# Differential attention on one Trainium2 core: another order of the same work on four engines, and 12 of 40 copies per head moved from ScalarE to VectorE

## The reference

```python
def diff_attention(q, k, v, lam, subln_g, lambda_init):
    ...
    def block(args):                       # 128 queries at a time
        qi, idx = args
        q_chunk = (idx * Q_BLOCK + jnp.arange(Q_BLOCK)) // CHUNK
        sc = jnp.einsum('bhqd,bhkd->bhqk', qi, kt).astype(jnp.float32) * (HEAD_DIM ** -0.5)
        mask = key_chunk[None, :] <= q_chunk[:, None]
        sc = jnp.where(mask[None, None], sc, NEG)
        p = jax.nn.softmax(sc, axis=-1).reshape(b, h, 2, Q_BLOCK, s)
        a = p[:, :, 0] - lam * p[:, :, 1]
        return jnp.einsum('bhqk,bhkv->bhqv', a.astype(vt.dtype), vt)
    ...
    o = rms_norm(o, subln_g) * (1.0 - lambda_init)
```

## Time and profile before

| | us |
|---|---|
| median of 3 runs | 2486.18 (2485.43 to 2487.39) |
| the profiled execution | 2485.43, of which the span of the trace is 2483.6 |
| `diff_attn` in it, first scores to last norm | 598.5 to 983.9: 385.4 |
| head 1, from its first scores to those of head 2 | 690.1 to 783.8: 93.7 |

### The profile page before, as it was taken

How to read it: one execution, slowest core, us unless ns; L and a number is a source line. 1 busy time by engine, 2 the same in 40 slices (tenths; PEclk the granted TensorE clock), 3 DMA queues, 4 the chain that set the end, 5 groups by cost and what they waited for, 6 DMA issues and landing times.

```text
span 2483.6 us, 34874 instructions
## 1 busy us (share of the span) xinstructions
PE 2358.0 (95%) x11796; PEld 1962.1 (79%) x11796; DVE 1589.1 (64%) x3041; ACT 1216.3 (49%) x2779; POOL 692.9 (28%) x818
## 2 busy tenths in 40 slices
PE   8999989996989997999999999999999999999998
PEld 6888878885777776777788888888888888888886
DVE  6777776554888786434755465567686555455877
ACT  5566664333777776433533333345554333334444
POOL 2333342222677576355311110110001111111001
PEclk9999999998999999999999999999999999999999
DMA  5111123434233221658632223266773322326774
GB/s 189 43 58 58 58 73 115 137 122 157 65 102 108 61 80 52 228 179 275 219 145 90 103 109 107 85 217 215 259 250 112 113 106 94 106 94 247 238 261 147
DMA packets 222353, 340.08 MB, mean 137 GB/s; under 512 B 20576, under 2 KB 119904, under 8 KB 220384
## 3 DMA queue, kind: packets, MB, share of 16 engines
q1 hardware_dynamic: 222176, 337.86, 40.7%
HBM read 234.50 MB, written 103.28 MB: 136 GB/s over the span
## 4 chain that ended last, share of the span: by engine, by line
PE 54%; POOL 2%; DVE 1%; issue 1%; ACT 1%; DMA 1%; SPq 0%; POOLq 0%; ACTq 0%; DVEq 0%
PE ff_psum L2452 33%; PE ff_psum L2476 17%; PE ff_psum L1725 3%; PE ff_psum L1739 1%; POOL op_mt_lo L1510 0%; DMA op_w_raw<-in_w_out_dram 0%; DVE op_h_row L1662 0%; DVE op_y_norm L1654 0%; POOL op_odd L1547 0%; POOL op_odd L1544 0%; ACT op_odd L1609 0%; DMA ff_hop<-hop_s 0%; ACT op_w_hi L1624 0%; POOL op_x_rstd L165 0%; POOL op_y_rstd L165 0%
## 5 line engine op out<-in xcount | busy, mean ns | idle before, releaser
L2452 PE MATMUL ff_psum<-ff_hop,ff_a_hi 128*128 128x512 f32 x2464 | 759.9, 390 | 3.6 <-DVE ff_hop L2212 2.6
L2452 PEld LDWEIGHTS ff_psum<-ff_hop,ff_a_hi 128*128 128x128 f32 x2464 | 462.8, 188 | 101.0 <-issue 4.7
L2452 PE MATMUL ff_psum<-ff_hop,ff_a_lo 128*128 128x512 f32 x1232 | 480.1, 390 | 0.0
L2452 PEld LDWEIGHTS ff_psum<-ff_hop,ff_a_lo 128*128 128x128 f32 x1232 | 231.6, 188 | 48.2
L2476 PE MATMUL ff_psum<-ff_a_hi 128*128 128x512 f32 x604 | 235.0, 389 | 0.0
L2476 PE MATMUL ff_psum<-ff_a_lo,ff_a_hi 128*128 128x512 f32 x604 | 235.0, 389 | 0.0
L2476 PE MATMUL ff_psum<-ff_a_hi,ff_a_lo 128*128 128x512 f32 x604 | 235.0, 389 | 0.0
L2078 ACT ACTIVATE ff_a_hi<-ff_w_raw 128x512 fp32r<-128x512 f32 x220 | 137.9, 629 | 193.6 <-PE ff_psum L2452 190.1
L2205 DVE TENSOR_TENSOR ff_a_lo<-ff_w_raw,ff_a_hi 128x512 fp32r<-128x512 f32 x220 | 163.3, 744 | 90.7 <-ACT ff_a_hi L2078 90.7
L1210 ACT ACTIVATE da_probs<-da_psum,da_bias 128x512 f32<-128x512 f32 (+3 forms) x320 | 195.9, 625 | 49.8 <-DVE da_bias L1262 45.6
L2033 POOL TENSOR_TENSOR ff_go<-ff_go 128x512 f32<-128x512 f32 x22 | 28.4, 1292 | 654.9 <-DVE ff_go L2286 635.0
(11 more groups left out here) (238 smaller groups left out, 4987.7 us busy)
## 6 DMA issues: line engine op xcount, KB each, us to landing
g_s<-ff_go SPq DMA_DIRECT2D x154, 256.0 KB, 2.0
ff_ring<-g_s SPq DMA_DIRECT2D x154, 256.0 KB, 2.8
ff_ring<-in_w_down_dram SPq DMA_DIRECT2D x132, 256.0 KB, 3.2
ff_w_raw<-in_w_gate_dram SPq DMA_DIRECT2D x44, 512.0 KB, 3.4
ff_w_raw<-in_w_up_dram SPq DMA_DIRECT2D x44, 512.0 KB, 3.5
pp_x<-in_x_dram SPq DMA_DIRECT2D x32, 512.0 KB, 4.3
ff_hop<-hop_s SPq DMA_DIRECT2D x14, 1024.0 KB, 7.6
hop_s<-op_odd SPq DMA_DIRECT2D x8, 1280.0 KB, 5.6
```

The lines of the kernel that those rows point to most:

```text
L2452: last = pe.matmul(ps[:, bank, :], w[:, unit % R, at], hop[i][:, h, c, :], start=(i in (0, 1, 6) and c == 0 and x_ == 0), stop=(c == 3 and ...
```

## The change

Three things change, all in `attention_plan` and what reads it.

1. `COPIED_BY` goes from H, H, H, G to H, G, H, G: the copy of chunk 1 is made by DVE, not by ACT. A head has 12 such copies, 9 of 512 columns and one each of 384, 256 and 128.
2. The shifts of `KINDS` and the costs in `us=` are other numbers, and in the plan P no longer comes behind N of two steps before (in the program it still waits for it). So the order on all four engines is another.
3. The plan is made for 3 heads. From its second head and the part of it that reaches beyond the start of the third, one head's order is cut out, and played for every head; pieces that reach into the next head carry the mark 1 (`ago`).

```diff
 KINDS = {
-    "S": ("PE", (-2.39, -1.12)),
-    "R": ("DVE", (1.04, 0.1)),
+    "S": ("PE", (-1.33, -1.82)),
+    "R": ("DVE", (-0.33, 0.02)),
...
 }
 COMBINED_BY = ("A", "B", "A", "B")
-COPIED_BY = ("H", "H", "H", "G")
+COPIED_BY = ("H", "G", "H", "G")
...
-    hop, own = 0.16, 0.05
+    heads, hop, own = 3, 0.16, 0.06
...
-    for h in range(DH):
+    for h in range(heads):
...
-            add("C", h, s, us=0.46, after=[("E", h, s, m, c) for m in range(2) for c in range(n)])
+            add("C", h, s, us=0.6, after=[("E", h, s, m, c) for m in range(2) for c in range(n)])
...
-                    us=1.85 * part[c] + 0.25 if combine == "A" else 0.98 * part[c] + 0.1)
+                    us=1.75 * part[c] + 0.3 if combine == "A" else 0.56 * part[c] + 0.1)
...
-            add("P", h, s, us=0.3, after=[("V", h, s, n - 1), second_last[0] >= 0 and ("N", *second_last)])
+            add("P", h, s, us=0.25, after=[("V", h, s, n - 1)])
...
-    order = sorted(start, key=lambda e: start[e])
+    begin = start["S", heads - 1, 0, 0, 0]
+    late = {(kind, *rest) for (kind, h, *rest), t in start.items() if h == heads - 2 and t >= begin}
+    order = []
+    for kind, h, *rest in sorted(start, key=lambda e: start[e]):
+        if h == heads - 2 and (kind, *rest) in late:
+            order.append((1, kind, *rest))
+        elif h == heads - 1 and (kind, *rest) not in late:
+            order.append((0, kind, *rest))
     return tiles_in_turn, chunks, order
...
         def heads(eng, perform):
 
-            for kind, h, *rest in order:
-                perform(h, kind, *rest)
+            for event in order:
+                if event[0] == 0:
+                    perform(0, *event[1:])
+            for h in range(1, DH):
+                for ago, *event in order:
+                    perform(h - ago, *event)
+            for ago, *event in order:
+                if ago:
+                    perform(DH - 1, *event)
```

More of the change, by code:

```diff
@@ L915 @@
 KINDS = {
-    "S": ("PE", (-2.39, -1.12)),
-    "R": ("DVE", (1.04, 0.1)),
[L918 to L929, removed]
+    "S": ("PE", (-1.33, -1.82)),
+    "R": ("DVE", (-0.33, 0.02)),
+    "M": ("DVE", (-1.55,)),
+    "E": ("ACT", (1.72, -2.49)),
+    "C": ("DVE", (-2.37,)),
+    "A": ("POOL", (0.0,)),
+    "B": ("DVE", (1.29,)),
+    "T": ("PE", (0.04,)),
+    "H": ("ACT", (0.17,)),
+    "G": ("DVE", (0.17,)),
+    "V": ("PE", (1.59,)),
+    "P": ("DVE", (1.31,)),
+    "Q": ("ACT", (-0.38,)),
+    "N": ("POOL", (1.3,)),
 }
 COMBINED_BY = ("A", "B", "A", "B")
-COPIED_BY = ("H", "H", "H", "G")
+COPIED_BY = ("H", "G", "H", "G")
 def attention_plan():
@@ L961, in attention_plan @@
                 for c in range(n):
-                    add("S", h, s, m, c, us=max(0.455 * part[c], 0.28) + 0.03, after=[slot("E", "S", S_SLOTS)])
-                    add("R", h, s, m, c, us=0.53 * part[c] + (0.21 if c == n - 1 else 0.13), after=[("S", h, s, m, c)])
-                add("M", h, s, m, us=0.1, after=[("R", h, s, m, c) for c in range(n)])
+                    add("S", h, s, m, c, us=max(0.43 * part[c], 0.32), after=[slot("E", "S", S_SLOTS)])
+                    add("R", h, s, m, c, us=0.53 * part[c] + (0.34 if c == n - 1 else 0.07), after=[("S", h, s, m, c)])
+                add("M", h, s, m, us=0.08, after=[("R", h, s, m, c) for c in range(n)])
                 for c in range(n):
@@ L1012, in diff_attn @@
     ordinal, total = {}, {}
-    for kind, _, *rest in sorted(e for e in order if e[1] == 0):
-        ordinal[(kind, *rest)] = total[kind] = total.get(kind, 0) + 1
+    for _, *e in sorted(order, key=lambda e: (e[2], e[0])):
+        ordinal[tuple(e)] = total[e[0]] = total.get(e[0], 0) + 1
     S_BANKS, T_BANKS, O_BANK = range(S_SLOTS), range(S_SLOTS, S_SLOTS + T_SLOTS), S_SLOTS + T_SLOTS
@@ L1278, in perform @@
                         cols = slice(4 * P * c, 4 * P * c + width(s, c))
-                        if c == COMBINED_BY.index("B"):
+                        if c == 1:
                             dve.wait_ge(factor_ready, h * steps + s + 1)
```

10 lines of the change are left out of this document (5 added, 5 removed).

## The result

| | before | after |
|---|---|---|
| median of 4 runs each, us | 2486.18 (2485.43 to 2487.39) | 2509.13 (2507.82 to 2510.15) |
| ratio, 95% interval | | 1.009, 1.0076 to 1.0105 |
| the profiled execution; its span | 2485.43; 2483.6 | 2507.67; 2505.9 |
| `diff_attn`, first scores to last norm | 385.4 | 404.4 |
| one head, from the C of its step 13 to the next head's, where the clock did not fall | 93.7 | 98.1 |

The forecast was 2494 (2480 to 2504). The direction was right and had 0.50. The size was off by 15 us, and the time lies near the rival that had 0.15 ("DVE's queue is crossed twice and falls further behind", 2507).

The account below looks back on a forecast made before the run. No engine is full; a ring of waits between engines sets the pace. Rounds 5 to 13 add 2.2 us in four heads (8.8), three changes of heads take 1.2: 7.6, say 8, giving 2494 (2480 to 2504).

Parts of the forecast that it names:

- DVE's queue is crossed twice and falls further behind: Rival, chance 0.15: all copies stay on the path, 5.2 us per head longer, 20.8 in all, 2507.
- rounds 5 to 9: A round runs from one step's C to the next; these five in each head were to get 2.1 us longer.
- rounds 10 to 13: Stretch of each head to the C of step 13: +0.3, -0.1, -0.8 and +0.7 us, together +0.1.
- the change of heads: Small steps between heads, three times, with POOL full: starts sooner, N(1) waits about 0.5 for Q(1), -0.4 in 25.8 us.
- the start: Start of the stage, up to the first head's rounds: costed at nothing, since step 0 waits for keys.
- The ring: C, DVE's B, R, M, ACT's E, then C: DVE's work between C and second M is on the path, later work hidden.
- The moved copies: 12 copies per head from ACT to DVE: 6.4 us more for DVE, free in waits, 0.60 each before the second M.
- The copies fall into waits and the rest evens out: Rival, chance 0.25: DVE's 16.3 us of waits per head take up the 6.4 of copies; time 2486.

Follow-up runs that it names:

- runs 3 and 4: One needless 512-column reduction added on DVE in 8 steps per head of before: ahead of the second M (3) 2499.6 us, behind it (4) 2488.2 us.
- run 9: Before with its order kept on all engines, but the 12 copies of chunk 1 made by DVE, each at a chosen place in its queue: 2493.9 us.
- run 8: After with the 12 copies on DVE cut to 128 columns, queue, order and waits unchanged: 2504.5 us.
- run 5: Before with POOL's two instructions of A replaced by memsets of about the same lengths, which read nothing: 2472.8 us.
- run 6: After with POOL's two instructions of A replaced by memsets of about the same lengths, which read nothing: 2495.7 us.
- run 14: Before with POOL's N(11) moved ahead of A(13; 0) and N(15) ahead of A(1; 0), as after has them: 2493.2 us.
- run 7: After with B(9; 3) and G(9; 1) put back behind M(10; 1), and A(1; 0) ahead of N(15): 2503.4 us.
- runs 1 and 2: 1: after with chunk 1 copied by ACT again, 2512.8 us; 2: before with chunk 1 copied by DVE and the plan of 3 heads, 2515.4 us.
- runs 10 to 12: New orders sought from measured distances: chunk 1 copied by ACT, own shifts 2476.8 us; by ACT, written list 2452.5 us; by DVE, written list 2459.3 us.
- run 13: After with S(8; 0, 1) and S(8; 0, 2) moved ahead of V(6; 2), and S(10; 0, 0) ahead of T(8; 2): 2500.8 us.

## Why the prediction was wrong

The stage was to be 7.6 longer and is 19.0 longer. By term: rounds 5 to 9 were put 2.0 too high; rounds 10 to 13 were missed by 6.8, the change of heads by 4.2, the start by 1.5 and the clock by 1.5; the end gives 0.6 back.

- **The ring** was right in kind: runs 3 and 4 show that a piece costs ahead of the second M and not behind it. "All of 0.60 where they stand between C and the second M" was too much: run 3 paid about half, and nothing in rounds 4 and 10.
- **The moved copies.** The price of 0.60 each was right, and so was that not all of it is paid. Put with care they cost 7.3 us (run 9), and their length 5.0 of after's 23 (run 8). I had weighed the change as one of copies; the larger part, 15.6 us between run 9 and after, is the order of the same work.
- **Rounds 5 to 9** came out: +2.1 predicted, +1.6 measured, round 6 and 7 at 9.5 and 11.1 for 9.2 and 11.0. Round 5 got shorter, not longer.
- **Rounds 10 to 13 are the first step that failed**: "+0.3, -0.1, -0.8 and +0.7, together +0.1" were +0.9, +0.8, -0.9 and +1.1 (8.78, 7.00, 3.94, 4.48 against 7.85, 6.21, 4.87, 3.43). The signs of the last two were right. In the first two I carried B over at 1.10 or at its old duration, although the prediction itself names that B is 1.64 when it meets A. B(9; 3) and B(10; 1) meet it in the new order (1.37 for 0.49, 1.52 for 0.82). Without A's reads (runs 5 and 6) these rounds differ by 1.1 instead of 1.8, so this is 0.7 of the 1.7 missed. Putting B(9; 3) and G(9; 1) back gave the 0.6 expected. The cause of the other 1.0 stays open: without A's reads, round 11 is still 0.5 and round 13 still 1.1 longer.
- **The change of heads is the second**: "It starts a little sooner, but N(1) waits about 0.5 for Q(1): -0.4". N(1) waits 0.88, N(11) stands in front of A(13; 0) and waits 0.70 for its Q, so POOL, which I took as full there, has gaps; the prediction named that as what would make it wrong. POOL's order alone is +0.8 per change in before (run 14), and A(1; 0) put back ahead of N(15) in after gives 0.7 (run 7).
- **The start** was costed at nothing since step 0 waits for keys. That covers step 0 only, whose C comes 4.7 behind the first scores in both; the steps 1 to 4 of the first head stand in the new order like all others, and cost 1.5.
- **The clock** was not in the sum at all. Two falls instead of one cost 1.5. They came behind a wait of PE for A of 2.38, in two of four heads with the same wait; before's one came behind a wait for E of 1.18.
- **The range.** The prediction's own width, 14 us about 2494, reaches to 2508; it was stated as 2504, with no number for what was taken off. 2509.1 lies outside either.
- **The rivals.** "The copies fall into waits and the rest evens out" was right on the copies in rounds 5 to 9 of run 9, but the rest does not even out. The rival of 2507 had the right size for another reason: it laid all 6.4 per head to copies on the path, and run 8 finds 1.2 (5.0 in four heads), of 4.0 taken away.
- PE's wait for A goes along with a bad order here, but not always: 9.1 us in before, 25.0 to 28.4 in after and in runs 1 and 2, 1.4 to 6.2 in the three orders of runs 10 to 12. In run 9 it is 6.7, with a time 7.3 us longer than before's, and in run 13 still 24.6, with 9 us gained. It is not shown to be the cause.

## What to carry to other kernels

A change of a planner's numbers is a new order, and a part of it taken alone is a third one, so it can't be judged by undoing parts; compare single moves in a fixed order. When you walk through a new order, price an instruction that another engine can hold up, as A does B here, by what that engine is doing at its new place, not by its old mean, and look at full engines for gaps that the new neighbours bring. With durations, and delays from one engine to the next, read from the traces of this case, a search over single moves found an order 34 us faster than before, where the two plans given were 23 apart.

## What the runs showed of the hardware

- A B of 512 columns that starts while an instruction of A or the last of N runs on POOL ends 0.55 us after it (0.40, 0.27 and 0.15 for 384, 256 and 128 columns), and the POOL instruction behind it is held until about 0.13 before B's end. C's factor, of one column, ends 0.02 after A's addition (1.22 instead of 0.22). Without such meetings before takes 15.6 us less (run 5), and after too (run 6). B gets through as soon as the one instruction of POOL ends, not the pair that makes up A.
- PE busy for 1.39 of 3.50 us, then the granted clock at 0.50 for 3.4 us, with a T of that stretch at 1.12 where it takes 0.66 at 1.00: such a fall costs 1.4 to 1.5 us beside the wait. The same wait is followed by a fall in two of four heads in after; in run 1, each head has one fall.
